# Start addresses of the SBUF tiles of an encoder kernel: multiples of 128 and of 16 bytes instead of 32

## The reference

```python
# per layer l of 2 (256 tokens, width 1024, float32; rotary, masks and shapes left out)
h = rms_norm(x, g_mix[l])
qa, ka, va, cq, ckv, kr, qm, gates = jnp.split(h @ w_in[l], split_points, axis=-1)
y_a = window_gqa(...)            # windowed attention, 8 heads of 64, 2 kv heads, sink logit
y_b = latent_attention(...)      # 8 heads, low-rank q and kv through w_uq, w_ukv
y_m = memory_attention(qm, mem_n, w_mem_kv[l])   # 4 heads into 256 memory tokens
mixed = (g[:, :, 0] * (y_a @ w_branch[l, 0]) + g[:, :, 1] * (y_b @ w_branch[l, 1])
         + g[:, :, 2] * (y_m @ w_branch[l, 2]))
x = x + mixed @ w_out[l]
h = rms_norm(x, g_ffn[l])
# l = 0: x = x + (silu(h @ w_gate) * (h @ w_up)) @ w_down                  (width 3584)
# l = 1: the same with the two best of 8 experts for each token, weighted by the router
...
return rms_norm(x, g_final)
```

## Time and profile before

| what | value |
|---|---|
| median of 3 runs (lowest, highest) | 1810.45 us (1808.38, 1810.64) |
| the profiled execution's own time | 1810.18 us |
| its span, first to last instruction | 1808.4 us |
| mean granted clock of TensorE | 0.993 |
| busy: PE, DVE, ACT, POOL | 97%, 77%, 66%, 1% |
| HBM traffic | 478 MB, 265 GB/s over the span |

### The profile page before, as it was taken

How to read it: one execution, slowest core, us unless ns; L and a number is a source line. 1 busy time by engine, 2 the same in 40 slices (tenths; PEclk the granted TensorE clock), 3 DMA queues, 4 the chain that set the end, 5 groups by cost and what they waited for, 6 DMA issues and landing times.

```text
span 1808.4 us, 28962 instructions
## 1 busy us (share of the span) xinstructions
PE 1754.6 (97%) x9812; PEld 1511.7 (84%) x9812; DVE 1389.7 (77%) x1506; ACT 1189.8 (66%) x1419; POOL 23.6 (1%) x49
## 2 busy tenths in 40 slices
PE   7999999999999999989999999999999999999997
PEld 6888899999988888878888888888888888788886
DVE  6675475455466755689989899899899899898996
ACT  5465544444445655467777777777777778777775
POOL 2000000000000000000000000000000000000000
PEclk9999999999999999989999999999999999999999
DMA  8544366666655434869989999999999899899990
GB/s 324 161 117 117 120 231 189 186 186 185 185 179 161 114 108 136 291 222 369 374 308 373 346 334 371 335 347 371 325 358 372 312 369 371 308 374 343 334 372 24
DMA packets 213867, 479.20 MB, mean 265 GB/s; under 512 B 14768, under 2 KB 16832, under 8 KB 213296
## 3 DMA queue, kind: packets, MB, share of 16 engines
q1 hardware_dynamic: 212592, 474.80, 75.9%
q0 software_dynamic: 1216, 3.61, 0.7%
HBM read 475.20 MB, written 3.15 MB: 265 GB/s over the span
## 4 chain that ended last, share of the span: by engine, by line
PE 89%; ACT 4%; issue 3%; DVE 3%; DMA 0%; POOLq 0%; POOL 0%; ACTq 0%; DVEq 0%
PE ps L1651 81%; PE ps L2021 2%; PE ps L2054 1%; PE ps L1878 1%; ACT probs L1003 1%; PE ps L1861 1%; PE ps L1848 1%; ACT whi L868 1%; PE ps L1703 1%; PE ps L1850 0%; DVE wlo L1176 0%; ACT probs L995 0%; DMA gain<-in_g_mem 0%; DVE act_m L1599 0%; ACT gates L1036 0%
## 5 line engine op out<-in xcount | busy, mean ns | idle before, releaser
L1176 DVE TENSOR_TENSOR wlo<-raw,whi 128x1024 fp32r<-128x1024 f32 x766 | 915.1, 1219 | 304.6 <-ACT whi L868 274.4
L868 ACT ACTIVATE whi<-raw 128x1024 fp32r<-128x1024 f32 x766 | 797.2, 1055 | 328.0 <-PE ps L1651 317.9
L1651 PE MATMUL ps<-whi,xg_hi 128*128 128x512 f32 x896 | 358.2, 400 | 2.4 <-DVE xg_lo L1182 2.4
L1651 PE MATMUL ps<-wlo,xg_hi 128*128 128x512 f32 x896 | 352.1, 393 | 0.0
L1651 PE MATMUL ps<-whi,xg_lo 128*128 128x512 f32 x896 | 349.8, 390 | 0.0
L1651 PE MATMUL ps<-hT_hi,whi 128*128 128x256 f32 x896 | 258.1, 288 | 4.2 <-ACT gates L878 2.9
L1651 PE MATMUL ps<-hT_lo,whi 128*128 128x256 f32 x896 | 252.9, 282 | 0.0
L1651 PE MATMUL ps<-hT_hi,wlo 128*128 128x256 f32 x896 | 252.3, 282 | 0.0
L1651 PEld LDWEIGHTS ps<-wlo,xg_hi 128*128 128x128 f32 x896 | 168.9, 188 | 38.6
L1651 PEld LDWEIGHTS ps<-whi,xg_hi 128*128 128x128 f32 x896 | 169.2, 189 | 38.0 <-DVE wlo L1176 5.4
L1651 PEld LDWEIGHTS ps<-whi,xg_lo 128*128 128x128 f32 x896 | 169.1, 189 | 35.3
(11 more groups left out here) (313 smaller groups left out, 2200.7 us busy)
## 6 DMA issues: line engine op xcount, KB each, us to landing
raw<-in_w_down_exp SPq DMA_DIRECT2D x200, 512.0 KB, 5.1
raw<-in_w_gate_exp SPq DMA_DIRECT2D x184, 512.0 KB, 4.9
raw<-in_w_up_exp SPq DMA_DIRECT2D x160, 512.0 KB, 5.3
raw<-in_w_in SPq DMA_DIRECT2D x72, 512.0 KB, 3.7
kM<-in_w_up_exp SPq DMA_DIRECT2D x40, 512.0 KB, 5.6
raw<-in_w_gate_dense SPq DMA_DIRECT2D x28, 512.0 KB, 4.4
raw<-in_w_up_dense SPq DMA_DIRECT2D x28, 512.0 KB, 4.3
raw<-in_w_down_dense SPq DMA_DIRECT2D x28, 512.0 KB, 4.2
```

The costliest lines, as they stand in the source:

```text
L868: s.activation(whi[n % SPLIT][:, 0:w], raw[tile(key)][:, 0:w], ACT.Copy).then_inc(chunk_hi, 1)
L1176: v.tensor_tensor(wlo[n % SPLIT][:, 0:w], raw[tile(key)][:, 0:w], whi[n % SPLIT][:, 0:w].bitcast(F32), ALU.subtract).then_inc(chunk_split, 1)
L1651: ins = mm(o, lhsT, rhs, start=start and i == 0, stop=stop and i == 2, skip_group_check=True)
```

## The change

`sb_in` now returns a function that asks for an alignment with every tensor: 128 bytes where a partition holds 128 elements or more, 16 bytes where it holds fewer. PSUM tensors and everything else stay as they are.

```diff
+import math
 from contextlib import ExitStack
...
         def sb_in(scope):
-            return lambda name, shape, dt=F32: scope.enter_context(nc.sbuf_tensor(name, shape, dt))
+            def tensor(name, shape, dt=F32):
+
+                line = 128 if math.prod(shape[1:]) >= 128 else 16
+                return scope.enter_context(nc.sbuf_tensor(name, shape, dt, align_bytes=line))
+            return tensor
```

## The result

| | before | changed |
|---|---|---|
| median | 1809.41 us (4 runs, 1807.78 to 1810.64) | 1822.43 us (4 runs, 1819.58 to 1823.64) |
| ratio, changed to before | | 1.0071, 95% interval 1.0056 to 1.0086 |
| span of the profiled execution | 1808.4 us | 1820.4 us |
| the same, its own time | 1810.18 us | 1822.17 us |

The prediction was 1806.0 us with a range of 1788 to 1814. The kernel became slower by 13 us, so the range missed it and the direction was wrong.

A forecast was written before the change was run, and what follows sets the result against it. TensorE was taken to bound both trunk and expert loop. The profiled 1810.18 us minus 4.4 us for the trunk's 512-wide matmuls, all other terms zero, gave 1805.8, or 1806.0 us on the median's scale; range 1788 to 1814.

The forecast's parts named there:

- TensorE sets the time, so only its step counts; ACT, DVE and DMA give nothing.: Whole kernel: only TensorE instruction lengths move the end; address changes on ACT, DVE and DMA were taken as nothing.
- The address of the stationary tile is the cause of 234 against 229 ns.: 512-wide matmuls: stationary tiles 96 past 128, not 64-byte aligned, cost 5.3 ns more each than those 64 past.
- The trunk's term, 828 x 5.3 = 4.4 us.: 828 matmuls 512 wide, with hT, actT, mixT, memT, ckvT stationary: gain 4.4 us, bounds 0 and 17.6 us.
- The expert loop's term: 4032 matmuls whose stationary tile goes from 64 to 0 past 128: taken as 0, bounds 21.4 us either way.
- The rival "slower": Expert loop: both operands at 0 past 128 meet, costing 21.4 us; 1831.9 us, or 1827.4 with the trunk's gain; chance 0.13.
- The rule of the Trainium skill on lines of 16 bytes: All SBUF reads: a penalty per 16-byte line crossed; every start stays a multiple of 16, so 1810.4 us, no change.
- The row with cqT, 384 wide,: Trunk matmuls with cqT stationary at 96 past: 173.2 ns steps, 13 ns over their columns, listed as evidence against the forecast.
- About 1080 us: Expert loop's length, used in the rival of a larger gain to call 21.4 us 2% of it; that rival's chance 0.13.
- Rival H: Trunk, forecast for e8: clock drops come with memT's or actT's address or shorter steps; one or both return, 1797 to 1799 us.

The follow-up runs named there:

- e1: Changed kernel with only the expert loop's stationary tiles back at their old place, 320 past a multiple of 512; 1806.56 us, ratio to before 0.9981.
- e2: Kernel before with 192 bytes of padding ahead of xg_hi and nothing else; 1824.0 us, ratio to before 1.0077.
- e8: Kernel before with padding of 320 bytes ahead of xg_hi and 416 ahead of mixT_hi and of actT_hi0; 1799.4 us, ratio 0.994.
- e4: Changed kernel with eight small tiles placed ahead of raw0, moving whi and wlo by 128 bytes, and 256 bytes padding ahead of xg_hi; 1802.76 us in one run.
- e3: Changed kernel with 128 bytes of padding ahead of xg_hi; 1800.19 us, ratio to before 0.994.
- e9: Kernel before, padded so xg_hi and actm_lo lie at distance 0 behind whi modulo 256, xg_lo and actm_hi at 96; 1819.28 us in one run.
- e7: Kernel before with 320 bytes of padding ahead of xg_hi and nothing else; 1803.71 us, ratio to before 0.9964.
- e5: Changed kernel padded so xg, actm, mixT, actT, memT start 32, 64, 160, 224, 128 bytes behind whi modulo 512; 1826.49 us in one run.
- e6: Changed kernel padded so xg, actm, mixT, actT, memT start 256, 448, 320, 288, 416 bytes behind whi modulo 512; 1803.7 us in one run.

## Why the prediction was wrong

- *TensorE sets the time, so only its step counts; ACT, DVE and DMA give nothing.* Right. Their rows did not move, and e1 shows that the aligned raw tiles neither gain nor cost.
- *The address of the stationary tile is the cause of 234 against 229 ns.* Half right. An address is the cause, but not its rest modulo 64. I had two points, 96 and 64 past 128, and drew a rule of alignment through them. What I had not done was to write down the moving operand's address beside each: whi starts at 128 past 512 in both, so the two points were also the distances 96 and 192.
- *The trunk's term, 828 x 5.3 = 4.4 us.* The sign was right and the step fell further, to 226.7 (7.6 ns; 6.3 us). The trunk still gave only 3.2 us. Two things lessen it. A piece needs five to ten matmuls to settle: in the dense loop after the change its second to fifth steps are 236, 228, 232 and 231 ns on average, before they come to 226.7. And in the profiled execution of the changed kernel the granted clock drops twice at places where it did not in that of the kernel before (last section). My estimate of their price from the timeline and the windows: 1.2 us at the first (six matmuls in 2.70 us instead of 1.47) and 1.4 us at the second (12 fewer matmuls of 120 ns in the same 12 us).
- *The expert loop's term: "I take 0, since 64 past is the nearest row".* This is the step that failed. It was the largest term of all, with bounds of 21.4 us either way, and I filled it with the nearest address instead of asking for a reason. Measured: 0.30 us on 72 matmuls, 4.2 ns each, 15.1 us on the loop. By distance modulo 256 the change moved these tiles from 192, the second best place, to 128.
- *The rival "slower".* It named the place, the sign and nearly the price (1827.4 us with the trunk's gain; measured 1822.4), at a chance of 0.13. Its mechanism was upside down: it feared that both operands at the same place modulo 128 would meet, but the same place modulo 256 is the fastest of all, and after the change the two were 128 apart.
- *The rule of the Trainium skill on lines of 16 bytes ("SBUF — State Buffer", "Door 1: The DMA port swizzle").* All starts in all these kernels are multiples of 16, so the rule has one price for them, and the sum by it was 1810.4. The medians differ by up to 25 us (1824.0 in e2, 1799.4 in e8). The rule does not account for this effect.
- *The row with cqT, 384 wide,* at 13 ns over its columns, spoke against alignment as such. Its step was 173.2 ns at distance 96 and is the same at distance 0 after the change. I noted it and left the model as it was. With 256 columns the step is 120 ns on both sides too. The change moved these matmuls only between the distances 96 and 0, so this does not show that they are indifferent to it; e4 shows otherwise (last section).
- *Two readings.* "About 1080 us" for the expert loop is too long: from the first matmul with xg, at 785.09 us, to the end of the span it is 1023. And the earlier trace rows has the loop's clock from 1300 to 1600 us only, not at the stretch of the earlier trace rows. Neither moves the sum.

Gains and losses stay below the settled step times 4032. A stretch of 72 goes from 16.50 to 16.37 us in e3, and 8 x 7 such stretches make 7.3 us, of which the loop shows 6.6; for the change it is 56 x 0.30 = 16.8 us, of which 15.1 are there. Two of a turn's stretches are in fact broken off by the scatter and the turn's end, and each begins unsettled. That these beginnings are the whole of the rest is argued from the steps and was not tested by itself.

## What to carry to other kernels

Where TensorE is the bound and streams 512-wide fp32r matmuls back to back, with a new stationary tile for each, put the stationary tiles at the same place modulo 256 bytes as the moving ones; a pad of some hundred bytes was worth 0.4% here, and the wrong one cost 0.8%. Do not read an address effect from one operand alone: list the starts of both beside each step before a rule is made. And a term with wide bounds and no row must not be set to zero because zero is the middle; it deserves the largest share of the doubt.

## What the runs showed of the hardware that was not expected

**Two values of distance are fast.** At a distance of 0 modulo 256 a 512-wide matmul costs 226.7 ns, 13.3 ns over its 512 columns at 2.4 GHz. The 384-wide (173.2) and the 256-wide (120.0) pay the same 13 ns at distance 0 and at 96. The 512-wide pay 19 to 21 ns at six of the eight distances, and 16 at 192.

At distance 128 the narrower ones move too, which no theory above had foreseen. In e4 the 256-wide matmuls, with whi as stationary and hT as moving operand, take 28.50 us / 240 = 118.8 ns, where the earlier trace rows has 120.0. The small gain is in its other 256-wide pieces as well (118.7 to 119.2 ns). With cqT, 384 wide, they take 176.0 instead of 173.3; but e9, where cqT and whi lie as before, has 174.9, so that this one is less clear.

```profile
273.67 28.50 PE ps L1659 x240
```

**The clock drops at different places.** In the kernel before the granted clock is 1.00 in both stretches of these windows:

```profile
40.00:60.00 20.00, 17.54 (x76) 13.84 (x75) 15.57 (x30) 9.78 (x13) 0.22 (x1) 1.00 0.47 133
300.00:312.00 12.00, 10.67 (x84) 10.00 (x83) 8.03 (x7) 4.26 (x5) 0.00 (x0) 1.00 0.41 126
```

In the changed kernel it is 0.91 and 0.86: for some 3.4 us at each place TensorE runs at half of full speed, 1.2 GHz.

```profile
40.00:60.00 20.00, 17.54 (x72) 14.10 (x71) 15.25 (x31) 9.78 (x13) 0.21 (x1) 0.91 0.50 140
...
300.00:312.00 12.00, 10.67 (x72) 10.01 (x72) 7.64 (x7) 4.12 (x4) 0.00 (x0) 0.86 0.41 134
```

Ahead of the first drop the chain has 2.46 us without a matmul, in both kernels alike (from 40.59 us before, from 40.52 after). In e8, which has its memory values at distance 0 but hT at 96, only the second drop is there:

```profile
40.00:60.00 20.00, 18.61 (x80) 15.01 (x81) 17.32 (x32) 9.48 (x14) 0.22 (x1) 1.00 0.48 136
300.00:312.00 12.00, 10.68 (x72) 10.01 (x71) 8.12 (x7) 4.08 (x4) 0.00 (x0) 0.86 0.57 178
```

e2 and e7, whose trunk is that of before, have neither drop. e1 and e3, whose trunk is that of the changed kernel, have both. e5 and e6, with hT as in the changed kernel and memT padded, have the second alone. On these kernels alone it looks as if the fast distance brought the drops; but e4, where hT and memT keep the changed kernel's addresses and the distance is 128, with a step of 232.5 ns, has both as well:

```profile
40.00:60.00 20.00, 18.47 (x73) 14.94 (x74) 15.61 (x30) 8.94 (x13) 0.24 (x1) 0.91 0.45 126
300.00:312.00 12.00, 10.68 (x72) 10.01 (x71) 8.12 (x7) 3.47 (x4) 0.00 (x0) 0.86 0.48 153
```

Nor do the addresses alone bring them. In e9 every tile of the trunk lies as in the kernel before, and it has the first drop:

```profile
40.00:60.00 20.00, 18.74 (x74) 15.07 (x75) 15.68 (x29) 8.69 (x13) 0.22 (x1) 0.91 0.47 134
300.00:312.00 12.00, 10.68 (x83) 10.00 (x83) 8.04 (x7) 4.52 (x5) 0.00 (x0) 1.00 0.43 135
```

Likewise e2 and e7, which have the same trunk, differ from 758 to 770 us: the granted clock is 1.00 there in e2 and 0.86 in e7 and in the kernel before. And the eight runs of e1 have mean granted clocks between 0.989 and 0.993, with one set of addresses. So where the clock drops varies with the same addresses, and each kernel's places were read from one execution. The means still lean one way: 0.992 in all four runs of e3, 0.993 or 0.994 in all of e2, e7 and e8, and 0.991 to 0.994 in those of the kernel before. Whether that comes from the addresses, and how, the runs do not say. Rival H of e8 was right in so far as one drop came back.
